# Expert 0's input rows: from full fp32 one-hot products to products of the two parts of X

## The chip, the cores and the metric

One core of one Trainium2 chip runs the program. The metric is the device time of one execution in microseconds (us), as the median of several runs. The engines are TensorE (PE, with its weight loads shown apart as PEld), VectorE (DVE), ScalarE (ACT), GpSimd (POOL) and SyncE (SP, which here only issues transfers).

## The reference, cut to what matters

A batch of 512 tokens with 1024 features passes through four layers: two with attention and a mixture of experts, and two with recurrent mixers and a plain feed-forward net. The change touches the two expert layers. What they compute is

```python
x = layer_norm(x * DN_ALPHA + mixer_out)           # 512 x 1024, f32
group, expert = router(x)                           # top-2 of 32 experts for each token
rows_e = x[tokens that chose e]                     # at most 96 rows kept per expert on the fast path
y_e = (silu(rows_e @ w_gate[e]) * (rows_e @ w_up[e])) @ w_down[e]
x = layer_norm(x * DN_ALPHA + sum of weight * y_e)
```

## The kernel before

The 512 tokens lie in four tiles (t = 0 to 3) of 128 rows in the buffer `X`. Accuracy near full f32 is had from two "parts": a value is rounded by ACT into a part that TensorE takes in a single pass (type fp32r, `one_pass(...)` in the code), and DVE subtracts it from the value, which leaves the second part. Most large products are three single-pass products of such parts. Plain f32 operands are the other way: for such a product the trace has two weight loads and two matmul records per call.

The end of each attention layer is `mixer_out` on TensorE (line 2434). Its last chunk of output columns is done for tiles 0, 1, 2, then tile 0 is transposed (`turn_tile`, L2296), then the chunk is done for tile 3, tile 1 is transposed, the router's logits of tile 0 are formed (`logits`, L2405), tile 2 is transposed, and so on up to the logits of tiles 2 and 3. DVE adds the residual and normalises tile by tile (`residual`, L3163 to L3138; `norm_tile` waits for POOL's reciprocal root, L1025, after `mean_var`, L3126). ACT copies each transposed tile out of two PSUM banks in order (`tiles_T`, L1245); each engine runs its list strictly in order.

Routing comes next, for tiles 0, 1 (q = 0) and then tiles 2, 3 (q = 1): DVE chooses (`choose`, L3403 to L3440), TensorE counts positions (`positions`, L2416, L2417), DVE places (`place`, L3449 to L3468) and writes a one-hot matrix `M["sel"]` of 128 x 96 per tile. `first_rows` (L2429) multiplies X by it, which gives expert 0's rows already transposed in banks 0 and 1, 16 calls for each q; so expert 0 needs no gather. `positions(l, 1)` stands behind `first_rows(l, 0)` in TensorE's list. ACT and DVE take the two banks out in two parts (L1484, L3611), and TensorE starts expert 0's first products (`up_first`, L2081, L2082, L2086), which free the weight halves for the next loads of SP (L906).

The rows of the other experts go through DRAM: POOL scatters X (L1051) and, once DVE's list `used` is ready (L3523), gathers the rows of experts 1, 2 and so on into `M["XE"]` (L1065), two buffers in turn. `clear_rows` (L1058) zeroes both of them; it runs while the mixer's last chunks are under way.

Of the kernel before, what the change touches and what calls it, by code (L numbers as in the profile page):

```python
# [7 lines left out]
ALU = mybir.AluOpType  # L8
ACT = mybir.ActivationFunctionType
# [183 lines left out]
def build(nc, a, out, stages=99):  # L193
    table, where = shape_constants()
    ctx = ExitStack()
    with ctx:
# [429 lines left out]
        M = carve([("XE", (2, D)), ("XET", (2, KD, P)), ("hid", (2, D_EXPERT)), ("YE", (2, D))], 8192)  # L626
        M["XN"] = M["XET"]
        M["XET"] = M["XET"][:, :, :, 0:CAP]
        M["XET_lo"] = XH[:, 0:2, :].rearrange("p b (k c) -> p b k c", k=KD)[:, :, :, 0:CAP]
        M["HT_lo"] = XH[:, 2:4, 0:KE * P].rearrange("p b (k c) -> p b k c", k=KE)[:, :, :, 0:CAP]  # L630
        M["HN"] = XH[:, 2:4, KE * P:2 * KE * P].rearrange("p b (k c) -> p b k c", k=KE)
        M["HT"] = M["HN"][:, :, :, 0:CAP]
        M["both"] = big[:, 15360:15360 + P]
        M["sel"] = big[:, 12288:12288 + T * CAP].rearrange("p (t c) -> p t c", t=T)
# [380 lines left out]
        def _(pool):  # L1015
# [45 lines left out]
            def rows_through(l):  # L1061
# [8 lines left out]
                def scatter(e):  # L1070
# [5 lines left out]
                    ).then_inc(signal(f"y_stored{e % 2}").sem, 16)  # L1076

                pool.wait_ge(signal("used_ready").sem, l + 1)
                pool.wait_ge(signal("rows_sent").sem, 16 * T * TOP_K * (l + 1))
# [40 lines left out]
            if on(3):  # L1120
                pool.wait_ge(full[U["o0_T"][KD - 1].bank], U["o0_T"][KD - 1].n + 1)
                norm_params(a["ln1_g"][0], a["ln1_b"][0])
                clear_rows()
                for t in range(T):
                    norm_rstd(t)
# [9 lines left out]
            if on(5):  # L1135
                pool.wait_ge(full[U["o1_T"][KD - 1].bank], U["o1_T"][KD - 1].n + 1)
                norm_params(a["ln1_g"][1], a["ln1_b"][1])
                clear_rows()
                for t in range(T):
                    norm_rstd(t)  # L1140
# [54 lines left out]
        def _(act):  # L1195
# [44 lines left out]
            def tiles_T(name):  # L1240

                for i, u in enumerate(U[name]):
                    t, b = divmod(i, 2)
                    act.wait_ge(full[u.bank], u.n + 1)
                    act.activation(XT[:, 4 * b:4 * b + 4, t * P:(t + 1) * P], ps(u)[:, :].rearrange("p (k c) -> p k c", k=4), ACT.Copy).then_inc(  # L1245
                        drained[u.bank], 1)
                    act.wait_ge(drained[u.bank], u.n + 1)

            def moments(t):
# [474 lines left out]
            if on(5):  # L1724
                linear("qkv", C["H"], 3 * D, between=raw_bias)
                act.wait_ge(signal("x_normed").sem, signal("x_normed").next(act, 2 * T))
                windows()
                round_chunk(W["odd_o"][1])
                tiles_T("ln11_T")
            if on(6):  # L1730
                experts(1)
            if on(7):
                round_chunk(W["mix_in"][0])
                act.wait_ge(signal("x_normed").sem, signal("x_normed").next(act, T))
                moments(0)
# [304 lines left out]
        def _(pe):  # L2040
# [379 lines left out]
            def first_rows(l, q):  # L2420

                base = U[f"moe{l}"]
                pe.wait_ge(signal("first_marked").sem, signal("first_marked").next(pe))
                for b in range(2):
                    if q == 0:
                        pe.wait_ge(drained[b], base[b])
                    for j in range(4):
                        for t in (2 * q, 2 * q + 1):
                            ins = pe.matmul(psum[b][:, j * CAP:(j + 1) * CAP], X[:, t, :].rearrange("c (h p k) -> c h k p", h=2, k=4)[:, b, j, :], M["sel"][:, t, :],  # L2429
                                            start=(t == 0 and j == 0), stop=(t == T - 1 and j == 3))  # L2430
                    if q == 1:
                        ins.then_inc(full[b], 1)
# [637 lines left out]
        def _(dve):  # L3070
# [87 lines left out]
            def residual_tile(name, c, t, scale):  # L3158
# [5 lines left out]
                dve.wait_ge(drained[u.bank], u.n + 1)  # L3164

            def residual(name, scale):

                for c in range(2):
                    for t in range(T):
                        residual_tile(name, c, t, scale)  # L3170
                        half_stats(t, c)
                        if c == 1:
                            mean_var(t)
                            norm_tile(t)

# [267 lines left out]
            def place(l, q):  # L3443
# [7 lines left out]
                for t in (2 * q, 2 * q + 1):  # L3451
                    ins = dve.tensor_scalar(M["sel"][:, t, :], k("places"), neg_mean[:, t:t + 1], R["M"][:, t, 0:1], ALU.is_equal, ALU.mult)
                ins.then_inc(signal("first_marked").sem, 1)
# [116 lines left out]
            def route(l):  # L3570

                dve.memset(R["LP"], -3e38).then_inc(dve_done.sem, 1)
                dve.wait_ge(dve_done.sem, dve_done.next(dve))
                dve.memset(R["Mc"][:, 0, :], 0.0).then_inc(dve_done.sem, 1)
                dve.wait_ge(dve_done.sem, dve_done.next(dve))
                for q in range(2):
                    choose(l, q)
                    place(l, q)
                scores(l)
                fullest(l)  # L3580
# [731 lines left out]
```

## Time and profile before

| | |
|---|---|
| median of 3 runs | 2994.32 us (2990.87 to 2997.32) |
| the profiled execution | 2994.94 us, of which the span of instructions is 2993.1 us |
| PE / PEld / DVE / ACT / POOL busy | 97% / 75% / 71% / 54% / 12% |
| mean granted TensorE clock | 0.982 |
| transfers | 600.5 MB, mean 201 GB/s |

Busy shares are means over stages with different limits. The granted clock is 1.00 at 2.4 GHz and 0.50 at 1.2 GHz. In a timeline a row may stand for several like instructions that follow each other; then its duration is that of all of them.

### The profile page before, as it was taken

How to read it: one execution, taken by the hardware profiler on the slowest of the kernel's cores; microseconds unless marked ns; L12 is line 12 of the kernel's file. 1: busy time of each engine (PE TensorE's matmuls, PEld its weight loads, DVE VectorE, ACT ScalarE, POOL GpSimd, SP SyncE). 2: the span in 40 equal slices, each digit the busy share in tenths (PEclk: the TensorE clock that was granted, in tenths of full speed). 3: DMA queues.
4: the chain of work that ended last, by engine and by line, in shares of the span. 5: the costliest groups of instructions: out<-in, count | busy, mean ns of one | idle time of the engine just before them, and what ended most of it. 6: DMA issues, size and time to landing. Idle time of an engine off the chain costs nothing.

```text
span 2993.1 us, 38811 instructions
## 1 busy us (share of the span) xinstructions
PE 2895.8 (97%) x14261; PEld 2257.0 (75%) x14261; DVE 2123.5 (71%) x2376; ACT 1604.9 (54%) x1969; POOL 358.4 (12%) x273
## 2 busy tenths in 40 slices
PE   8999899999989999899999999999999999999998
PEld 7668776767768767677677668888888887888886
DVE  3485799999972467899999865674776648676762
ACT  3573588888853464788888743433222226522211
POOL 0000212222220002122222220100000000000000
PEclk9999899999999998999999999999999999999999
DMA  7303799999962125899999844301232223232222
GB/s 273 136 1 113 261 389 405 409 398 400 405 223 85 39 99 226 334 399 398 404 399 406 332 106 99 66 20 64 92 102 95 99 85 99 92 111 93 91 94 84
DMA packets 170900, 600.50 MB, mean 201 GB/s; under 512 B 21697, under 2 KB 71025, under 8 KB 121363
## 3 DMA queue, kind: packets, MB, share of 16 engines
q1 hardware_dynamic: 140432, 541.22, 48.5%
q0 software_dynamic: 19840, 52.60, 4.9%
q10 hardware_dynamic: 10499, 4.91, 0.6%
q8 instruction: 88, 1.44, 0.2%
q14 instruction: 41, 0.34, 0.0%
HBM read 574.15 MB, written 40.37 MB: 205 GB/s over the span
## 4 chain that ended last, share of the span: by engine, by line
PE 73%; DMA 11%; DVE 7%; ACT 5%; issue 3%; POOL 1%; DVEq 0%; SPq 0%; ACTq 0%; POOLq 0%
PE bank L2074 14%; PE bank L2076 14%; PE bank L2075 14%; DMA ring<-w_gate 6%; PE bank L2512 4%; PE bank L2509 4%; DMA ring<-w_up 3%; PE bank L2086 3%; PE bank L2794 2%; PE bank L2528 2%; PE bank L2081 2%; PE bank L2082 2%; PE bank L2138 1%; PE bank L2139 1%; ACT ring_rounded L1479 1%
## 5 line engine op out<-in xcount | busy, mean ns | idle before, releaser
L3601 DVE TENSOR_TENSOR ring_rounded<-ring,big_rounded 128x2048 fp32r<-128x2048 f32 x252 | 567.6, 2288 | 32.0 <-ACT big_rounded L1479 31.0
L1479 ACT ACTIVATE big_rounded<-ring 128x2048 fp32r<-128x2048 f32 x252 | 481.9, 1916 | 44.2 <-DMA ring<-w_up 33.2
L3096 DVE TENSOR_TENSOR ring_rounded<-ring,ring_rounded 128x2048 fp32r<-128x2048 f32 (+2 forms) x118 | 261.4, 2255 | 329.8 <-ACT ring_rounded L1221 329.4
L1221 ACT ACTIVATE ring_rounded<-ring 128x2048 fp32r<-128x2048 f32 (+2 forms) x124 | 226.5, 1876 | 369.3 <-DMA ring<-ffn_w_down 150.1
L3601 DVE TENSOR_TENSOR ring_rounded<-ring,ring_rounded 128x2048 fp32r<-128x2048 f32 x128 | 292.4, 2288 | 43.5 <-ACT ring_rounded L1479 43.1
L1479 ACT ACTIVATE ring_rounded<-ring 128x2048 fp32r<-128x2048 f32 x128 | 245.0, 1917 | 96.5 <-DMA ring<-w_gate 95.5
L2074 PE MATMUL bank<-XT_rounded,ring_rounded 128*128 128x512 f32 (+1 forms) x792 | 295.8, 374 | 0.4 <-DVE XH_rounded L3149 0.4
L2076 PE MATMUL bank<-XT_rounded,ring_rounded 128*128 128x512 f32 (+1 forms) x792 | 292.9, 370 | 0.0
L2075 PE MATMUL bank<-XH_rounded,ring_rounded 128*128 128x512 f32 (+1 forms) x792 | 292.9, 370 | 0.0
L2512 PE MATMUL bank<-ring_rounded,big_rounded 128*128 128x512 f32 x960 | 265.7, 399 | 7.4 <-DVE ring_rounded L3601 6.9
L2075 PE MATMUL bank<-ring_rounded,XH_rounded 128*64 128x512 f32 (+2 forms) x608 | 239.6, 394 | 0.0
L2076 PE MATMUL bank<-ring_rounded,big_rounded 128*128 128x512 f32 (+1 forms) x608 | 235.8, 388 | 0.0
L2512 PEld LDWEIGHTS bank<-ring_rounded,big_rounded 128*128 128x128 f32 x960 | 179.2, 190 | 59.5 <-DVE ring_rounded L3601 22.5
L2074 PE MATMUL bank<-ring_rounded,XT_rounded 128*128 128x512 f32 (+1 forms) x560 | 218.6, 390 | 0.4 <-DVE XH_rounded L4043 0.3
L2075 PE MATMUL bank<-ring_rounded,XT_rounded 128*128 128x512 f32 (+1 forms) x560 | 217.0, 387 | 0.0
L2074 PE MATMUL bank<-big_rounded,XH_rounded 128*64 128x512 f32 (+1 forms) x496 | 199.1, 401 | 5.1 <-DVE XH_rounded L3615 5.1
L2076 PE MATMUL bank<-big_rounded,XH_rounded 128*64 128x512 f32 (+1 forms) x512 | 202.4, 395 | 0.0
L3720 DVE SCALAR_TENSOR_TENSOR big<-bank,chan,big 128x511 f32<-128x511 f32 (+2 forms) x236 | 176.7, 749 | 8.4
L1073 POOL DMA_INDIRECT expert_rows<-big,idx x64 | 88.1, 1377 | 766.4 <-ACT big L1515 739.9
L1023 POOL TENSOR_SCALAR st<-st 128x1 f32<-128x1 f32 (+3 forms) x43 | 14.5, 337 | 1302.7 <-ACT lnp L1589 801.1
L2074 PEld LDWEIGHTS bank<-XT_rounded,ring_rounded 128*128 128x128 f32 x792 | 149.3, 188 | 26.3 <-issue 1.6
L2075 PEld LDWEIGHTS bank<-XH_rounded,ring_rounded 128*128 128x128 f32 x792 | 149.3, 189 | 25.8 <-issue 1.0
(525 smaller groups left out, 5527.1 us busy)
## 6 DMA issues: line engine op xcount, KB each, us to landing
ring<-w_up SPq DMA_DIRECT2D x128, 1024.0 KB, 9.8
ring<-w_down SPq DMA_DIRECT2D x128, 1024.0 KB, 7.7
ring<-w_gate SPq DMA_DIRECT2D x128, 1024.0 KB, 7.9
ring<-ffn_w_up SPq DMA_DIRECT2D x44, 1024.0 KB, 7.0
ring<-ret_gdn_w_in SPq DMA_DIRECT2D x8, 2048.0 KB, 13.1
ring<-ffn_w_down SPq DMA_DIRECT2D x8, 2048.0 KB, 7.7
expert_rows<-lnp POOLq DMA_DIRECT2D x1, 12288.0 KB, 40.3
ring<-odd_w_qkv SPq DMA_DIRECT2D x6, 2048.0 KB, 8.1
```

The source lines that it names most:

```text
L1073: pool.indirect_dma_start(expert_rows, bass.IndirectOffsetOnAxis(ap=used[0:slots_of(e), e:e + 1], axis=0), M["YE"][0:slots_of(e), e % 2, : ...
L1221: act.activation(one_pass(hi(c)[:, ks, :]), raw(c)[:, ks, :], ACT.Copy).then_inc(rounded[c.pair], 1)
L1479: act.activation(one_pass(expert_hi(j)), expert_raw(j), ACT.Copy).then_inc(signal("half_rounded").sem, 1)
L2074: pe.matmul(dst, x_hi, y_hi, start=first, stop=False)
L2075: pe.matmul(dst, x_hi, y_lo, start=False, stop=False)
L2076: return pe.matmul(dst, x_lo, y_hi, start=False, stop=last)
L2086: return pe.matmul(dst, one_pass(x_hi), one_pass(y_lo), start=False, stop=last)
L2509: pe.matmul(psum[b][:, :], one_pass(M["XN"][:, half, 4 * i + kk, :]), one_pass(expert_hi(j)[:, kk, :]), start=(i + kk == 0), stop=False)
L2512: ins = pe.matmul(psum[b][:, :], one_pass(M["XN"][:, half, 4 * i + kk, :]), one_pass(expert_raw(j)[:, kk, :]), start=False, stop=(4 * i + ...
L3096: dve.tensor_tensor(one_pass(w), w, parts(hi(c)[:, ks, :]), ALU.subtract).then_inc(split[c.pair], 1)
L3601: dve.tensor_tensor(one_pass(expert_raw(j)), expert_raw(j), parts(expert_hi(j)), ALU.subtract).then_inc(signal("half_split").sem, 1)
L3720: ins = dve.scalar_tensor_tensor(dst[:, d:S], ps(u)[:, 0:S - d], taps[n - 1 - d], dst[:, d:S], ALU.mult, ALU.add)
```

## The change

ACT rounds each normalised tile of X into a first part `x_hi` (`x_rounded`), and DVE takes the rest into `x_lo` (`x_rest`). The parts lie in buffers that are not yet used at that time (the two row buffers `XE` among them). The one-hot matrix is written as fp32r, and each plain f32 call of `first_rows` becomes two single-pass calls, one for each part. `x_rounded(t)` stands in ACT's list ahead of the copies of tile t for t = 0, 1, 2, and behind all copies for t = 3. `x_rest(t - 1)` stands in DVE's list between `mean_var(t)` and `norm_tile(t)`; `x_rest(3)` stands between `choose(l, 1)` and `place(l, 1)`. Since `XE` now holds parts of tile 2, `clear_rows` moves: POOL runs it after both banks of `first_rows` are complete, ahead of the first gather.

```diff
+        M["XET_all"] = M["XET"].rearrange("p b k c -> p b (k c)")
+        M["x_hi"] = [M["XET_all"][:, 0], M["YE"][:, 0], M["XE"][:, 0], XH[:, 2, :]]
+        M["x_lo"] = [M["XET_all"][:, 1], M["YE"][:, 1], M["XE"][:, 1], XH[:, 3, :]]
@@ POOL, rows_through
+                for b in range(2):
+                    pool.wait_ge(full[b], base[b] + 1)
+                clear_rows()
                 pool.wait_ge(signal("used_ready").sem, l + 1)
@@ POOL, ahead of norm_rstd, both layers
-                clear_rows()
@@ ACT, tiles_T
                 for i, u in enumerate(U[name]):
                     t, b = divmod(i, 2)
+                    if b == 0 and t < T - 1:
+                        x_rounded(t)
                     act.wait_ge(full[u.bank], u.n + 1)
...
+                x_rounded(T - 1)
+
+            def x_rounded(t):
+                act.wait_ge(signal("x_normed").sem, signal("x_normed").next(act))
+                act.activation(one_pass(M["x_hi"][t]), X[:, t, :], ACT.Copy).then_inc(signal("x_rounded").sem, 1)
@@ PE, first_rows
+                pe.wait_ge(signal("x_rest").sem, signal("x_rest").next(pe, 2))
...
-                            ins = pe.matmul(psum[b][:, j * CAP:(j + 1) * CAP], X[:, t, :].rearrange("c (h p k) -> c h k p", h=2, k=4)[:, b, j, :], M["sel"][:, t, :],
-                                            start=(t == 0 and j == 0), stop=(t == T - 1 and j == 3))
+                            for part, rows in enumerate((M["x_hi"][t], M["x_lo"][t])):
+                                ins = pe.matmul(psum[b][:, j * CAP:(j + 1) * CAP], one_pass(rows.rearrange("c (h p k) -> c h k p", h=2, k=4)[:, b, j, :]), one_pass(M["sel"][:, t, :]),
+                                                start=(t == 0 and j == 0 and part == 0), stop=(t == T - 1 and j == 3 and part == 1))
@@ DVE
+            def x_rest(t):
+                dve.wait_ge(signal("x_rounded").sem, signal("x_rounded").next(dve))
+                dve.tensor_tensor(one_pass(M["x_lo"][t]), X[:, t, :], parts(M["x_hi"][t]), ALU.subtract).then_inc(signal("x_rest").sem, 1)
@@ DVE, residual
                             mean_var(t)
+                            if t:
+                                x_rest(t - 1)
                             norm_tile(t)
@@ DVE, route
                     choose(l, q)
+                    if q == 1:
+                        x_rest(T - 1)
                     place(l, q)
```

## Rows read from the trace of the kernel before

**Rows 1.** The profile's page: engine shares of the chain that ended last.

```profile
PE 73%; DMA 11%; DVE 7%; ACT 5%; issue 3%; POOL 1%; DVEq 0%; SPq 0%; ACTq 0%; POOLq 0%
```

**Rows 2.** Chain that ended last, first expert layer: start us, us, what.

```profile
297.26 0.43 PE bank L2416 x2
298.84 7.78 PE bank L2429 x32
306.63 0.43 PE bank L2416 x2
308.35 7.78 PE bank L2429 x32
318.07 0.43 PE bank L2082
342.69 8.27 DMA ring<-w_gate
```

**Rows 3.** Stretches: length; busy (instructions) of PE, PEld, DVE, ACT, POOL; PEclk; DMA share, GB/s.

```profile
299.20:299.40 0.20, 0.20 (x2) 0.20 (x2) 0.20 (x1) 0.20 (x1) 0.00 (x0) 0.83 0.00 0
321.00:323.00 2.00, 2.00 (x7) 1.25 (x6) 2.00 (x2) 0.00 (x0) 1.70 (x2) 0.50 0.22 43
323.00:325.00 2.00, 2.00 (x10) 1.44 (x9) 2.00 (x1) 0.00 (x0) 0.84 (x1) 0.94 0.44 111
400.00:500.00 100.00, 97.83 (x450) 70.62 (x449) 91.05 (x61) 85.72 (x81) 24.13 (x12) 0.98 1.01 400
```

**Rows 4.** Groups by form (weights 128*128, moving 128x96 and so on): count, busy us, mean ns, idle.

```profile
L2521 PE MATMUL bank<-big 128*128 128x512 f32 x120 | 61.2, 591 | 0.0
L2512 PE MATMUL bank<-ring_rounded,big_rounded 128*128 128x512 f32 x960 | 265.7, 399 | 7.4 <-DVE ring_rounded L3601 6.9
L2405 PE MATMUL bank<-router,XT 128*128 128x36 f32 x128 | 14.8, 275 | 0.0
L2405 PEld LDWEIGHTS bank<-router,XT 128*128 128x128 f32 x128 | 14.8, 192 | 0.0
L2512 PEld LDWEIGHTS bank<-ring_rounded,big_rounded 128*128 128x128 f32 x960 | 179.2, 190 | 59.5 <-DVE ring_rounded L3601 22.5
L2075 PEld LDWEIGHTS bank<-ring_rounded,XH_rounded 128*64 128x64 f32 x480 | 64.7, 135 | 40.4
```

**Rows 5.** DVE's timeline, first expert layer, the norm of tile 3 and the start of place(0, 1).

```profile
288.23 0.21 DVE L3126 BATCH_NORM_AGGREGATE st<-st 128x2 f32<-128x12 f32 x1
289.52 1.28 DVE L3136 SCALAR_TENSOR_TENSOR X<-X,st,lnp 128x1024 f32<-128x1024 f32 x1 [1.08 <-POOL st L1025]
307.53 0.16 DVE L3449 COPY st<-bank 128x2 f32<-128x2 f32 x1 [2.73 <-PE bank L2417]
```

**Rows 6.** ACT's timeline, first expert layer: copies of tile 1, the route's exponential.

```profile
287.19 1.23 ACT L1245 ACTIVATE XT<-bank 128x512 f32<-128x512 f32 x2 [5.24 <-PE bank L2296]
309.79 0.22 ACT L1464 ACTIVATE st<-st 128x16 f32<-128x16 f32 x1 [4.69 <-DVE st L3480]
```

**Rows 7.** Groups by form: ACT and DVE passes of 128x1024 into fp32r.

```profile
L1221 ACT ACTIVATE ring_rounded<-ring 128x1024 fp32r<-128x1024 f32 x4 | 4.2, 1060 | 23.4 <-DMA ring<-ffn_w_down 23.4
L3096 DVE TENSOR_TENSOR ring_rounded<-ring,ring_rounded 128x1024 fp32r<-128x1024 f32 x4 | 4.9, 1226 | 13.8 <-ACT ring_rounded L1221 13.8
```

**Rows 8.** PE's timeline around the last tile: transposes of tile 1, transposes of tile 3.

```profile
286.50 1.04 PE L2296 MATMUL bank<-const,X 128*128 128x128 f32 x8
292.18 1.09 PE L2296 MATMUL bank<-const,X 128*128 128x128 f32 x8 [0.32 <-DVE X L3138]
```

**Rows 9.** POOL's and PE's timeline: clearing, gather, its transposes; landing of L1065's gathers.

```profile
243.13 1.83 POOL L1058 MEMSET big<- 96x2048 f32 x1
319.31 2.38 POOL L1065 DMA_INDIRECT big<-expert_rows,idx  x1 [4.22 <-DVE idx L3523]
331.16 1.08 PE L2464 MATMUL bank<-const,big 96*128 96x96 f32 x8
DMA to landing us min/median/max: 4.1/8.8/9.8
```

More of the change, by code:

```diff
@@ L1137, in _ @@
                 norm_params(a["ln1_g"][1], a["ln1_b"][1])
-                clear_rows()
                 for t in range(T):
@@ L1725, in _ @@
                 linear("qkv", C["H"], 3 * D, between=raw_bias)
-                act.wait_ge(signal("x_normed").sem, signal("x_normed").next(act, 2 * T))
+                act.wait_ge(signal("x_normed").sem, signal("x_normed").next(act, T))
                 windows()
@@ L1733, in _ @@
                 round_chunk(W["mix_in"][0])
-                act.wait_ge(signal("x_normed").sem, signal("x_normed").next(act, T))
                 moments(0)
@@ L3451, in place @@
                 for t in (2 * q, 2 * q + 1):
-                    ins = dve.tensor_scalar(M["sel"][:, t, :], k("places"), neg_mean[:, t:t + 1], R["M"][:, t, 0:1], ALU.is_equal, ALU.mult)
+                    ins = dve.tensor_scalar(one_pass(M["sel"][:, t, :]), k("places"), neg_mean[:, t:t + 1], R["M"][:, t, 0:1], ALU.is_equal, ALU.mult)
                 ins.then_inc(signal("first_marked").sem, 1)
```

## The prediction

> **What bounds the kernel now.** I read the page first: TensorE carries 73% of the chain that ended last, transfers 11% [rows 1]. The change touches two short stretches, one in each expert layer, so the chain is read there next. It runs through `first_rows`: 32 records in 7.78 us for q = 0, the positions of q = 1, which stand behind them on TensorE, 32 records in 7.78 us again, then, once ACT and DVE have taken the banks out, `up_first` [rows 2]. The second expert layer repeats this within 0.1 us, so each term below counts twice. Behind it the weights' stream is the bound: the chain turns to a transfer of `w_gate` at 342.69 [rows 2], and the DMA share is 1.01 from 400 to 500 [rows 3]. That stream starts when `up_first` frees the first half, so whatever moves the start of `up_first` moves the whole expert stage, one for one.
>
> Next the granted clock, by stretches. It falls from 1.00 to 0.50 between 299.2 and 299.4 and returns after 323 [rows 3]. So nearly all of `first_rows` runs at 1.2 GHz, and so do the first 13 or so records of `up_first` (0.43 us for a record of 512 columns [rows 2]). TensorE had done its last dense 512-column product before 286.5 [rows 8]; since then it had done only transposes, 36-column logits and the positions.
>
> **The products themselves.** Before, 16 f32 calls for each q leave 32 records. After, 16 calls become 32 single-pass calls, so 32 records. What does one cost? Before: 7.78 / 32 = 0.243 us [rows 2]. Is that the passes or the weight load? The moving side is 96 columns. Plain f32 does pass twice in a record: with 512 columns a record has 591 ns against 399 ns for a single-pass one, 192 ns more, about 512 columns more at 2.4 GHz [rows 4]. But with 36 columns a record still takes 14.8 / 128 = 0.116 us at full clock [rows 4], although two passes of 36 columns are 0.03 us: there the load of 128 weight columns is the floor. Doubled for the half clock that is 0.23, next to the 0.243 seen, while two passes of 96 columns are 0.16 us at 1.2 GHz. The positions, with unbroken weights, take 0.43 / 2 = 0.215 us at the same clock [rows 2]. So the record is bound by the load. And the load of an fp32r weight is no shorter: 190 ns for 128 columns against 192 ns for f32; 64 columns take 135 ns [rows 4], so a column costs (190 - 135) / 64 = 0.86 ns, two cycles, 110 ns for 128 columns, 220 ns at half clock. No row has an fp32r product with so few columns, so I bound it: from 0.215 (positions) to 0.243 us, and I take 0.243, since it has the same stepped weights. Saved by the passes: nothing; at the lower bound 32 x 0.028 = 0.9 us for each q.
>
> A rule weighed: the Trainium skill (FP8 and Floating Point Precision, TensorE Precision Notes) counts true FP32 as four passes, so two parts against one exact operand would be half. The 591 ns of the wide record agree with it, the 0.116 us of the narrow one shows where it stops to matter; what it would give is rival A.
>
> **What is added, and where it lies.** ACT: four `x_rounded` of 128x1024 per layer at 1.06 us; DVE: four `x_rest` at 1.23 us [rows 7].
> - x_rest(0) stands where DVE waits 1.08 us for POOL's root in any case; it costs some 0.2 us, and DVE's wait for the next tile's product takes that up.
> - x_rest(2), ahead of norm_tile(3), is the one that counts. It needs x_rounded(2), and that stands in ACT's list behind the copies of tile 1, which wait for TensorE's transposes at 286.50 and run from 287.19 for 1.23 us, to 288.42 [rows 6, 8]. So x_rounded(2) ends at 288.42 + 0.03 + 1.06 = 289.51. DVE is ready for x_rest(2) at 288.23 + 0.21 = 288.44 [rows 5] and waits; it runs 289.56 to 290.79, and the norm of tile 3 starts at 290.83 instead of 289.52 [rows 5]: **+1.31 us**. POOL's root is ready long before. x_rest(1) suffers the same wait, 1.3 us, but DVE's idle time ahead of the residual of tile 3 and its wait for x_rounded(2) take it up.
> - Queued behind that wait on DVE is all of the routing: the norm of tile 3, `choose`, `place`. TensorE waits with it, for tile 3's transposes at 292.18 [rows 8]. Nothing in between has slack: DVE goes from `choose` to `place` waiting only for the positions.
> - x_rest(3), 1.23 us, lies in the 2.73 us that DVE waits for the positions of q = 1 [rows 5]. Cost nothing; without that cover, 1.23 us.
> - x_rounded(3) moves ACT's later weight rounding by 1.06 us; ACT then idles 4.69 us ahead of the exponential [rows 6]. Nothing.
> - `clear_rows` leaves POOL's list ahead of the norms, where it was off the path. In its new place it starts at the end of the products, 308.35 + 7.78 = 316.1 [rows 2], and takes 1.83 us, to some 318.1; the gather waits for DVE's list in any case and starts at 319.31. Its landing is needed by the transposes at 331.16 [rows 9]. Behind it in POOL's list stand the gathers and scatters only. Nothing.
>
> Sum: 2 x 1.31 = 2.6 us more. On the profiled execution: 2994.94 + 2.6 = 2997.5; it lies 0.6 above the median of the three runs, 2994.32, and on that the forecast is **2997**.
>
> **Rivals.**
> A. *A record gets cheaper* because the passes decide after all. For: a wide f32 record does show its second pass. Against: the narrow rows above, and the load time of fp32r. Price: each q in 3.89 us. For q = 0, positions can start when `choose` ends, and DVE's wait shrinks from 2.73 to the 1.27 of x_rest(3): 1.46 saved. For q = 1 all 3.89. So 5.35 - 1.31 = 4.04 us for each layer, 8.1 in all: 2986. The Trainium skill (TensorE: Matmul & The Clock Gate, Fast Weight Load) would go further, with a quick load of 128 weights for types other than FP32; 190 ns for fp32r against 192 for f32 speaks against it. Chance 0.13.
>
> B. *The clock falls earlier*, the slower side. TensorE now has 0.32 us idle before tile 3's transposes [rows 8]; with the change 1.6 us. If the clock falls before the logits of tiles 2 and 3 (32 records behind those transposes, now 32 x 0.116 = 3.7 us), they take 32 x 0.215 = 6.9 us, from 294.4 to 301.3, and the positions of q = 0, wanted at 297.26 [rows 2] + 1.31 = 298.6, stand behind them: 2.7 us, and 0.2 for themselves at half clock. With the 1.31 that is 4.2 for each layer: 2994.3 + 8.4 = 3002.7. It decides if the clock falls more than about 2 us sooner than at 299.3. For: longer idleness ahead. Against: it fell 12.8 us after the last dense product [rows 3, 8], about the same in the second layer, and that product does not move. Chance 0.12.
>
> C. *The clock returns later* in `up_first`, since TensorE's array does less in `first_rows` (96 columns for each load, not 192). It returned some 5 to 6 us after the 512-column records began (the row at 318.07 is an early one [rows 2, 3]). A record of 512 columns costs 0.43 instead of 0.23, so each us later costs about 0.5; 3 us later in both layers gives 2997 + 3 = 3000. Chance 0.07.
>
> D. *The change does not hide its clearing*: POOL's memset beside DVE's busy stretch, or behind a late semaphore, delays the gather. A gather lands at most 9.8 us after its issue, so at 329.1, and is needed at 331.16 [rows 9]; it decides from 2 us late on. At 3 us late it gives 1 us for each layer: 2999. Chance 0.03.
>
> **How the numbers follow.** Forecast 0.65, A 0.13, B 0.12, C 0.07, D 0.03. A measurement of this kernel tells 0.2%, 6 us, from no change. Faster by more: A, 0.13. Slower by more, above 3000.3: B and part of C, 0.15. The rest, 0.72, is within. The forecast's own range is 2993 (0.9 us saved for each q in both layers, less 2.6) to 3000; run to run the kernel spreads by 3 us either way. The range over the cases leaves out most of A: 2987 to 3003.5.
>
> **What would show it.** In the changed profile: 32 records for each q in about 7.8 us at a granted clock of 0.50; DVE idle about 1.1 us ahead of x_rest(2), released by ACT; norm of tile 3 starting 2.6 us behind `mean_var` rather than 1.3; DVE's wait ahead of `place(l, 1)` reduced by x_rest(3) to about 1.5 us; the memset ending before the list is ready. The prediction is wrong if the records come at 0.12 to 0.16 us, or if the clock falls before the positions.

## The result, and the profile after

The changed kernel took 3002.96 us (median of 7 runs, 2999.92 to 3013.06), the kernel before beside it 2991.59 us (7 runs): a ratio of 1.0032, 95% interval 1.0021 to 1.0043, or 9.6 us more (the medians themselves are 11.4 us apart; the sums below go by the ratio). The profiled execution took 3003.21 us (span 3001.4) against 2994.94 before, 8.3 us more. The forecast of 2997 was some 6 us short; the range (to 3003.5) just holds the median, because it took in the slower rival B, and the loss is over the 0.2% that a measurement tells.

Line numbers moved: the transposes are L2308, the logits L2417, the positions L2428 and L2429, `first_rows` L2443, expert 1's transposes L2478, the norm L3150 and L3152, POOL's two small operations for the root L1026 and L1028. New are `x_rounded` (ACT, L1260) and `x_rest` (DVE, L3183).

TensorE's timeline of the changed kernel, first expert layer, tile 1's transposes, then tile 3's and what follows (start us, us, engine line, tile, count, idle time before and its releaser):

```profile
286.48 1.04 PE L2308 MATMUL bank<-const,X 128*128 128x128 f32 x8
...
293.36 1.09 PE L2308 MATMUL bank<-const,X 128*128 128x128 f32 x8 [1.52 <-DVE X L3152]
294.29 5.93 PE L2417 MATMUL bank<-router,XT 128*128 128x36 f32 x32
300.03 0.67 PE L2428 MATMUL bank<-big,ones 128*128 128x64 f32 x2
```

Tile 1 is where it was, within 0.02 us [rows 8]. Tile 3's transposes come 1.18 us later and TensorE idles 1.52 us ahead of them, not 0.32. Then the logits of tiles 2 and 3 (32 records) take 5.93 us, where the forecast wanted 3.7, and the positions start 2.77 us later than before [rows 2]. The stretches of the granted clock say why (columns as in [rows 3]):

```profile
295.00:295.20 0.20, 0.20 (x4) 0.20 (x4) 0.17 (x2) 0.20 (x1) 0.03 (x1) 1.00 0.00 0
295.20:295.40 0.20, 0.20 (x4) 0.20 (x3) 0.17 (x2) 0.17 (x2) 0.00 (x0) 0.80 1.01 184
295.40:295.60 0.20, 0.20 (x3) 0.20 (x2) 0.17 (x2) 0.20 (x1) 0.00 (x0) 0.50 0.43 123
```

It fell to 1.2 GHz at 295.3, four us sooner than before, and in the middle of the logits. The second expert layer is worse. TensorE's timeline there; it had done its last dense product at 1145.92:

```profile
1153.30 1.97 PE L2308 MATMUL bank<-const,X 128*128 128x128 f32 x8 [2.02 <-DVE X L3152]
```

and the clock, which fell at 1152.1, while TensorE idled ahead of those transposes:

```profile
1151.90:1152.10 0.20, 0.00 (x0) 0.00 (x0) 0.16 (x2) 0.00 (x0) 0.00 (x0) 0.91 0.48 205
1152.10:1152.30 0.20, 0.00 (x0) 0.00 (x0) 0.20 (x1) 0.00 (x0) 0.00 (x0) 0.50 1.54 655
```

The transposes take 1.97 instead of 1.09 us, and the logits behind them 6.88 instead of 3.66. The products themselves are as they were: the chain of waits of the changed kernel has 7.75 us for each q, against 7.78 [rows 2].

```profile
302.05 7.75 PE bank L2443 x32
...
311.53 7.75 PE bank L2443 x32
```

The second thing that the forecast did not have stands in the timelines of DVE and POOL. DVE, first expert layer, the norm of tile 3:

```profile
288.88 0.21 DVE L3140 BATCH_NORM_AGGREGATE st<-st 128x2 f32<-128x12 f32 x1
289.54 1.25 DVE L3183 TENSOR_TENSOR big_rounded<-X,big_rounded 128x1024 fp32r<-128x1024 f32 x1 [0.45 <-ACT big_rounded L1260]
290.71 1.27 DVE L3150 SCALAR_TENSOR_TENSOR X<-X,st,lnp 128x1024 f32<-128x1024 f32 x1
```

Tile 3's norm starts at 290.71 (forecast 290.83). The same place one tile earlier starts at 284.79 with 0.44 us of waiting for POOL behind `x_rest(1)`, and POOL's rows for tiles 1 and 2 are:

```profile
276.62 1.15 POOL L1026 TENSOR_SCALAR st<-st 128x1 f32<-128x1 f32 x1 [4.75 <-DVE st L3140]
277.86 0.55 POOL L1028 TENSOR_TENSOR st<-st,const 128x1 f32<-128x1 f32 x1
282.90 0.19 POOL L1026 TENSOR_SCALAR st<-st 128x1 f32<-128x1 f32 x1 [4.50 <-DVE st L3140]
283.18 1.58 POOL L1028 TENSOR_TENSOR st<-st,const 128x1 f32<-128x1 f32 x1
```

Whichever of the two small operations starts while `x_rest` runs takes one us longer: 1.15 instead of 0.19, or 1.58 instead of 0.55. At tile 3 of this layer the second one starts at 289.52, just ahead of the pass, and takes 0.54 us.

`up_first` starts 3.14 us later in the first layer. In the second it starts 11.12 us later, of which 5.67 us were there at tile 1's transposes, so 5.45 us are new. Together 8.6 us, and the execution is 8.3 us longer.

### The profile page after: what moved, and what is told of

It reads as the page before. It is cut to its first block, busy times and chain, and to the rows that moved or that the text cites. A ratio compares the mean times of both kernels' runs of the same rounds, so it can differ in the third digit from the quotient of the medians.

```text
span 3001.4 us, 38830 instructions
## 1 busy us (share of the span) xinstructions
PE 2899.3 (97%) x14261; PEld 2260.9 (75%) x14261; DVE 2134.0 (71%) x2384; ACT 1613.1 (54%) x1977; POOL 359.5 (12%) x273
## 4 chain that ended last, share of the span: by engine, by line
PE 73%; DMA 10%; DVE 7%; ACT 5%; issue 4%; POOL 1%; DVEq 0%; SPq 0%; ACTq 0%; POOLq 0%
PE bank L2086 14%; PE bank L2088 14%; PE bank L2087 14%; DMA ring<-w_gate 6%; PE bank L2526 4%; PE bank L2523 4%; PE bank L2098 3%; DMA ring<-w_up 3%; PE bank L2542 2%; PE bank L2808 2%; PE bank L2093 2%; PE bank L2094 2%; ACT ring_rounded L1492 2%; PE bank L2150 1%; PE bank L2151 1%
## 5 line engine op out<-in xcount | busy, mean ns | idle before, releaser
L3624 DVE TENSOR_TENSOR ring_rounded<-ring,big_rounded 128x2048 fp32r<-128x2048 f32 x252 | 567.7, 2289 | 33.7 <-ACT big_rounded L1492 32.9
L1026 POOL TENSOR_SCALAR st<-st 128x1 f32<-128x1 f32 (+3 forms) x43 | 15.9, 370 | 1306.1 <-ACT lnp L1602 802.4
```

The costliest lines, as they stand in the source:

```text
L3624: dve.tensor_tensor(one_pass(expert_raw(j)), expert_raw(j), parts(expert_hi(j)), ALU.subtract).then_inc(signal("half_split").sem, 1)
```

## The experiments

Where an experiment's kernel starts its layer some us earlier or later, distances from the start of tile 1's transposes (the end of the last dense product) are compared. This table has the two expert layers of each profiled execution, and the ratio of all runs to the kernel before. "Fall" is the distance at which the granted clock fell, "tile 3" and `up_first` are starts. One execution stands for each kernel's distances: those of e1, e3 and e8 were the fastest of their runs, those of e5 and e13 among the slowest.

| kernel | tile 3 | fall | logits of tiles 2, 3 | `up_first` | ratio |
|---|---|---|---|---|---|
| before | 5.68 / 5.68 | 12.8 / 12.4 | 3.66 / 3.66 | 30.9 / 30.9 | 1 |
| the change | 6.88 / 7.38 | 8.8 / 6.1 | 5.93 / 6.88 | 34.0 / 36.3 | 1.0032 [1.0021, 1.0043] |
| e1_act_order | 7.16 / 7.31 | 6.9 / 8.1 | 6.88 / 6.88 | 36.1 / 35.5 | 1.0038 [1.0023, 1.0053] |
| e2_rest_late | 6.36 / 6.41 | 6.5 / 8.1 | 6.88 / 6.23 | 35.1 / 33.8 | 1.0023 [1.0013, 1.0033] |
| e3_split_only | 6.89 / 7.37 | 13.0 / 9.5 | 3.66 / 5.76 | 32.0 / 34.3 | 1.0024 [1.0014, 1.0035] |
| e4_products_only | 5.68 / 5.68 | 11.4 / 11.6 | 3.66 / 3.66 | 30.9 / 30.9 | 1.0001 [0.9991, 1.0011] |
| e5_one_part | 5.68 / 5.68 | 10.9 / 9.7 | 3.66 / 4.06 | 26.0 / 26.3 | 0.9961 [0.9948, 0.9975] |
| e8_after_dense_t3 | 6.88 / 7.37 | 12.6 / 11.7 | 3.66 / 3.82 | 31.9 / 32.9 | 1.0013 [1.0004, 1.0023] |
| e10_rests_moved | 5.78 / 5.84 | 10.3 / 11.7 | 3.66 / 3.66 | 31.4 / 31.4 | 1.0007 [0.9998, 1.0016] |
| e11_rest_beside | 6.57 / 6.56 | 7.8 / 6.1 | 6.59 / 6.88 | 34.2 / 35.3 | 1.0017 [1.0007, 1.0028] |
| e12_bf16_parts | 5.78 / 5.85 | 13.0 / 11.7 | 3.66 / 3.66 | 27.0 / 27.3 | 1.0019 [1.0008, 1.0029] |
| e13_bf16_filled | 5.78 / 5.85 | 10.2 / 11.7 | 3.68 / 3.66 | 27.0 / 27.3 | 1.0001 [0.9992, 1.001] |

### The split or the products: e3_split_only and e4_products_only

e3 keeps the split, its waits and the moved clearing, and forms the products in f32 as before. e4 does the reverse: no `x_rest` on DVE, and the second part is a buffer of zeros, so that the second part's share of expert 0's rows is left out.

```diff
 e3, PE, first_rows (and the one-hot stays f32)
-                            for part, rows in enumerate((M["x_hi"][t], M["x_lo"][t])):
-                                ins = pe.matmul(psum[b][...], one_pass(rows...), one_pass(M["sel"][:, t, :]), ...)
+                            ins = pe.matmul(psum[b][...], X[:, t, :]..., M["sel"][:, t, :], ...)
 e4, PE, first_rows (and both x_rest calls are gone)
-                            for part, rows in enumerate((M["x_hi"][t], M["x_lo"][t])):
+                            for part, rows in enumerate((M["x_hi"][t], M["x_lo"][0])):
```

> The changed kernel with its split, its clearing and all its waits, but with the products and the one-hot matrix in plain f32 as before. Theory W: same as the changed kernel, 3003 us, and the same early fall of the clock. Rival P (the products in fp32r cost): back towards 2992 to 2995 us.

> The single-pass products without the price of the split: DVE takes no rest; the second product of each pair reads a buffer of zeros instead of the rest, so expert 0's rows lack the second part of X. ACT still rounds, off the path. Theory W with the load as the floor of a record: 32 records for each q in 7.75 us as in both kernels, clock falls behind the logits, whole time that of the kernel before, 2992 us plus or minus 3. Rival A (passes decide): 3.9 us for each q and about 2981 us.

e3 took 3001.83 us and e4 2995.9 us, with the kernel before at 2994.43 beside them. e4's chain has the products at

```profile
302.55 7.75 PE bank L2447 x32
...
312.10 7.75 PE bank L2447 x32
```

So two single-pass records cost what one f32 call costs, the products change nothing, and the whole loss is the split and what waits for it. e4 also keeps the moved clearing, so that costs nothing either. Rival A is out. One part of e3's expectation missed: in its first layer the clock did not fall early (13.0 us, logits in 3.66 us).

### What a record costs: e5_one_part

e4 without its second part: 16 records for each q, and X's second part is left out of expert 0's rows.

```diff
-                            for part, rows in enumerate((M["x_hi"][t], M["x_lo"][0])):
+                            for part, rows in enumerate((M["x_hi"][t],)):
```

> The kernel with zeros for the rest (DVE takes none), with the second product of each pair left out: 16 records for each q; expert 0's rows have only the first part of X. Theory W with the weight load as the floor: 0.24 us a record at half clock, so 3.9 us for each q; for q = 0 DVE's wait ahead of place(1) shrinks by about 1.6, for q = 1 3.9 us are saved: 5.5 us for each layer, 2983 us. Rival (the clock returns later because TensorE does less): as much of it is lost in up_first, 2988 to 2992 us.

It took 2982.15 us, ratio 0.9961 [0.9948, 0.9975]. TensorE's timeline of this kernel:

```profile
302.95 3.97 PE L2447 MATMUL bank<-big_rounded 128*128 128x96 f32 x16 [0.93 <-DVE big_rounded L3475]
```

Half the records (0.248 us each) is half the time, and 12 us of the kernel. The stretch is worth attacking, then, but by the count of records (or what a record costs), which the change left at 32.

### ACT's wait: e2_rest_late and e1_act_order

e2 takes `x_rest(2)` away from tile 3's norm and puts it ahead of `x_rest(3)`. e1 leaves it, and has ACT round tile t + 1 ahead of the copies of tile t, so that the rounded tile is there in time.

```diff
 e2, DVE, residual (and route: x_rest(T - 2) ahead of x_rest(T - 1))
-                            if t:
+                            if t and t < T - 1:
                                 x_rest(t - 1)
 e1, ACT, tiles_T
-                    if b == 0 and t < T - 1:
-                        x_rounded(t)
+                    if b == 0 and t < T - 2:
+                        if t == 0:
+                            x_rounded(0)
+                        x_rounded(t + 1)
```

> The changed kernel, with the rest of tile 2 taken by DVE between choose(1) and place(1), not ahead of the norm of tile 3. Theory W (the loss is the wait ahead of the norm of tile 3, and the earlier fall of the clock that this idleness brings): tile 3's transposes start within 0.5 us of the kernel before (292.2 and, measured from tile 1's transposes, 5.7 us behind them), the clock falls behind the logits again, the logits of tiles 2 and 3 take 3.7 us and not 5.9 or 6.9, and the start of up_first comes 2 to 3 us earlier than in the changed kernel in the first layer, 4 to 5 us in the second: about 2993 to 2997 us. Rival P (the single-pass products or the late clearing cost the time): the whole time stays at 3003.

> The changed kernel with ACT rounding tile t + 1 ahead of the copies of tile t (for t = 0 and 1), so that x_rounded(2) no longer stands behind tile 1's copies. Theory W: x_rest(2) starts without the 0.45 us wait, but DVE's pass and POOL's root then start together, and POOL's root is slowed as it is ahead of the norm of tile 1 (0.7 us of wait left behind the pass), so the norm of tile 3 still starts some 2.1 us behind mean_var and not 1.3; the clock still falls early in at least one layer; 2999 to 3003 us. Rival (the wait on ACT is the whole delay): norm of tile 3 starts as before and the time is 2994.

e2 missed: 3001.05 us where the time of before was expected. The norm of tile 3 waits 1.08 us for POOL again, as before, yet tile 3 is still 0.7 us late. DVE's timeline shows what had come to it from the tiles ahead:

```profile
284.84 1.23 DVE L3183 TENSOR_TENSOR big_rounded<-X,big_rounded 128x1024 fp32r<-128x1024 f32 x1 [0.39 <-ACT big_rounded L1260]
286.50 1.28 DVE L3150 SCALAR_TENSOR_TENSOR X<-X,st,lnp 128x1024 f32<-128x1024 f32 x1 [0.44 <-POOL st L1028]
291.89 1.29 DVE L3150 SCALAR_TENSOR_TENSOR X<-X,st,lnp 128x1024 f32<-128x1024 f32 x1 [1.08 <-POOL st L1028]
```

In the kernel before, DVE's idle time ahead of tile 3's residual was

```profile
286.78 0.69 DVE L3163 SCALAR_TENSOR_TENSOR X<-X,bank 128x512 f32<-128x512 f32 x1 [1.07 <-PE bank L2076]
```

What tiles 1 and 2 lost to their passes and to POOL is more than these 1.07 us. In e1 DVE doesn't wait for ACT at tile 3, and still nothing is won (3004.65 us):

```profile
289.22 1.23 DVE L3185 TENSOR_TENSOR big_rounded<-X,big_rounded 128x1024 fp32r<-128x1024 f32 x1
291.15 1.28 DVE L3152 SCALAR_TENSOR_TENSOR X<-X,st,lnp 128x1024 f32<-128x1024 f32 x1 [0.71 <-POOL st L1028]
```

Without ACT's wait the pass falls on POOL's first operation, and DVE waits 0.71 us for POOL afterwards. ACT's wait and POOL's stall take each other's place.

### POOL beside DVE, by itself: e10_rests_moved and e11_rest_beside

e10 takes all passes off the norms. e11 differs from it in one thing: `x_rest(0)`, whose input was rounded long ago, stands between `mean_var(3)` and `norm_tile(3)`.

```diff
 e10, DVE, residual                              e11: x_rest(0) if t == 3, ahead of norm_tile(t)
-                            if t:
-                                x_rest(t - 1)
                             norm_tile(t)
+                            if t == 2:
+                                x_rest(0)
 both, DVE, route, between choose and place
-                    if q == 1:
-                        x_rest(T - 1)
+                    if q == 0:
+                        x_rest(1)
+                    else:
+                        x_rest(2)
+                        x_rest(3)
```

> The changed kernel with all of DVE's passes for the second parts taken off the norms: x_rest(0) stands behind norm_tile(2), where DVE waits 1.07 us for TensorE's product in the trace of before; x_rest(1) stands between choose and place of q = 0; x_rest(2) and x_rest(3) stand between choose and place of q = 1. ACT's roundings stay where they are. Theory (the loss is what stands ahead of tile 3's norm, in two portions: ACT's wait plus a POOL that is slow beside DVE's pass): tile 3's transposes come 5.7 to 5.9 us behind tile 1's, as before (5.68), POOL's two small operations take 0.19 and 0.55 us again, the norm waits 1.08 us, the clock falls 12 to 13 us behind the last dense product, the logits of tiles 2 and 3 take 3.7 us, and the kernel loses only what x_rest(1) lacks in cover, 0.5 to 1 us for each layer: ratio 1.0000 to 1.0008. Rival (ACT's roundings slow POOL or the copies too): tile 3 still comes over 0.5 us late and the ratio stays at 1.002 or above.

> As e10_rests_moved, but x_rest(0), whose input was rounded long ago, stands between mean_var(3) and norm_tile(3), so that one pass of DVE of 1.23 us, with no wait of its own, lies beside POOL's two small operations. Theory (a tensor_tensor pass of DVE holds POOL up for its length): POOL's first operation takes about 1.15 instead of 0.19 us or its second about 1.5 instead of 0.55, the norm of tile 3 still waits 0.7 us behind the pass and starts about 1.9 us behind mean_var instead of 1.08, so tile 3's transposes come 0.7 to 0.9 us late; the clock may fall earlier; ratio 1.000 to 1.002. Rival (POOL works beside it): the norm starts 1.25 us behind mean_var, tile 3 comes 0.15 us late.

e10: 2996.17 us against 2994.59, ratio 1.0007, as expected; the early fall is gone. e11: 2999.59 us, ratio 1.0017. POOL's timelines at tile 3, of e10 and then of e11:

```profile
288.89 0.19 POOL L1026 TENSOR_SCALAR st<-st 128x1 f32<-128x1 f32 x1 [5.70 <-DVE st L3140]
289.17 0.54 POOL L1028 TENSOR_TENSOR st<-st,const 128x1 f32<-128x1 f32 x1
```

```profile
288.42 1.15 POOL L1026 TENSOR_SCALAR st<-st 128x1 f32<-128x1 f32 x1 [5.60 <-DVE st L3140]
289.65 0.54 POOL L1028 TENSOR_TENSOR st<-st,const 128x1 f32<-128x1 f32 x1
```

and DVE's of e11:

```profile
288.29 1.23 DVE L3183 TENSOR_TENSOR big_rounded<-X,big_rounded 128x1024 fp32r<-128x1024 f32 x1
290.23 1.28 DVE L3150 SCALAR_TENSOR_TENSOR X<-X,st,lnp 128x1024 f32<-128x1024 f32 x1 [0.71 <-POOL st L1028]
```

One pass with no wait of its own costs 1.23 + 0.71 us where a wait of 1.08 us stood, 0.8 us net, and the logits took 6.6 and 6.9 us. That a pass beside POOL's small operations adds itself to them, rather than hiding them, is shown. In e10 ACT's roundings run as in the change, and POOL's operations are quick: it is DVE's pass, not ACT's.

### The clock: e8_after_dense_t3, e6_before_dense, e9_before_dense_all

e8 is the changed kernel with three plain f32 products of 256 columns, whose result nobody reads, in the idle time ahead of tile 3's transposes. e6 puts such products into the kernel before, ahead of the positions (one) and of the first `first_rows` (two); e9 fills every gap up to the second one.

```diff
+            def dense(l, n):
+                u = U[f"ln1{l}_T"][3]
+                pe.wait_ge(drained[u.bank], u.n + 1)
+                for _ in range(n):
+                    pe.matmul(ps(u)[:, 0:256], ident, const[:, 0:256], start=True, stop=True)
 e8, mixer_out
                 logits(l, 1)
+                dense(l, 3)
                 turn_tile(normed, X, 3, "x_normed")
 e6, mixer_out (e9: also 1 ahead of tile 3, 3 behind first_rows(l, 0), 1 ahead of first_rows(l, 1))
                 logits(l, 3)
+                dense(l, 1)
                 for q in range(2):
                     positions(l, q)
+                    if q == 0:
+                        dense(l, 2)
                     first_rows(l, q)
```

> The changed kernel with three plain f32 products of 256 columns (about 1.4 us of TensorE at full clock, results unused) between the logits of tile 1 and the transposes of tile 3, where TensorE idles 1.5 and 2.0 us. Theory W: the idleness is what makes the clock fall early, so with it filled the clock stays at 1.00 through the logits of tiles 2 and 3 (3.7 us) and up_first starts 2 us earlier in the first layer, 3 to 4 us in the second; about 2998 us. Rival (the clock falls at its time whatever TensorE does in this gap): logits still 5.9 and 6.9 us, 3003 us.

> The kernel before, with plain f32 products of 256 columns (0.47 us each at full clock, results unused): one between the logits of tile 3 and the positions of q = 0, two between these positions and first_rows(0), where TensorE waits for DVE. If dense work in these gaps holds the clock at 1.00 through first_rows(0), a record costs 0.12 us and up to 8 us for each layer are gained: 2980 us. If not (first_rows itself is too thin to hold it): 2992 to 2994 us.

> The kernel before with such products in every gap of TensorE from the logits on: one ahead of tile 3's transposes, one ahead of the positions, two ahead of first_rows(0), three behind it, one ahead of first_rows(1). If the clock stays at 1.00: up_first starts 6 to 9 us earlier than in the kernel before, 2978 to 2984 us. If it falls in spite of them, the three products behind first_rows(0) delay the positions of q = 1 by about 2.8 us: 2997 us.

e8 took 2998.47 us, ratio 1.0013. Its timeline of TensorE:

```profile
291.46 1.54 PE L2452 MATMUL bank<-const 128*128 128x256 f32 x6
293.15 1.09 PE L2308 MATMUL bank<-const,X 128*128 128x128 f32 x8
294.08 3.66 PE L2417 MATMUL bank<-router,XT 128*128 128x36 f32 x32
```

Tile 3 is as late as in the change (6.88 us behind tile 1), and the logits are back at 3.66 us. By the ratios 5.7 of the 9.6 us hang on the early fall (1.0032 less 1.0013; the intervals leave some 4 us to either side); by `up_first` in the profiled executions it is 5.5 (8.6 us late in the change, 3.1 in e8, whose profiled execution took 2994.78 us).

e6 (2994.83 us, ratio 1.0009) and e9 (2994.86 us, 0.9999) gained nothing. e9 tells why, for it holds `first_rows` at either level. Two stretches of it, the first within q = 0 and the second within q = 1:

```profile
302.20:306.20 4.00, 4.00 (x19) 4.00 (x19) 2.06 (x13) 2.67 (x2) 2.79 (x3) 0.50 0.90 358
311.20:315.20 4.00, 4.00 (x19) 4.00 (x18) 2.84 (x14) 0.92 (x3) 2.50 (x3) 1.00 0.36 145
```

19 records in 4 us at 1.2 GHz, and 19 in 4 us at 2.4 GHz. The weight loads of these records, grouped by form, give the same row in both stretches:

```profile
L2429 PEld LDWEIGHTS bank<-big,X 128*128 128x128 f32 x18 | 4.3, 329 | 0.0
```

329 ns a load at either level, where a load for the logits takes 192 ns at full clock [rows 4]. The chain of waits has the positions just ahead of the second at full speed, and 32 records of `first_rows` in 7.78 us as always:

```profile
308.81 0.19 PE bank L2416 x2
309.00 0.21 PE bank L2417 x2
...
310.13 7.78 PE bank L2429 x32
```

So these products don't run with the granted clock, and holding it through them gives nothing back. That fillers could save the logits in e8 is no contradiction: those take 0.116 us a record at one level and 0.215 at the other.

### A cheaper record: e12_bf16_parts and e13_bf16_filled

e12 is e10 with bf16 for both parts and the one-hot. It leaves out what two bf16 parts can't hold of a value of X for expert 0. e13 adds seven filler products ahead of expert 1's transposes.

```diff
 e12
-    one_pass(rows.rearrange("c (h p k) -> c h k p", h=2, k=4)[:, b, j, :]), one_pass(M["sel"][:, t, :])
+    half_width(rows, D).rearrange("c (h p k) -> c h k p", h=2, k=4)[:, b, j, :], half_width(M["sel"][:, t, :], CAP)
 e13, also, PE, rows_T
+                    if isinstance(e, int) and e == 1:
+                        wait_use(drained, 0, e)
+                        for _ in range(7):
+                            pe.matmul(psum[0][:, 0:256], ident, const[:, 0:256], start=True, stop=True)
```

> As e10_rests_moved, but both parts and the one-hot are bf16 instead of fp32r: ACT writes bf16(X), DVE writes bf16 of the rest. This leaves out what two bf16 parts can't hold of each value of X for expert 0 (the bits below some 16). Again 32 records for each q. It asks whether a record of these products is bound by the load of its 128 weight columns whatever the type. If a column costs the same two cycles: 7.7 us for each q, ratio as e10. If the narrower type loads in half the cycles, a record comes to about 0.12 us at the half clock (or to the 96 columns' own pass, 0.08 to 0.1 us at 1.2 GHz), first_rows takes 3 to 4 us for each q, and as with e5_one_part some 6 us for each layer come back: ratio about 0.996.

> As e12_bf16_parts (it leaves out the same: what two bf16 parts can't hold of X for expert 0), with seven plain f32 products of 256 columns (some 3.6 us at full clock) in front of expert 1's transposes, in the stretch in which TensorE waits for the gathered rows (4.93 us in the first expert layer, 3.67 in the second). In e12_bf16_parts TensorE reached that wait 3.9 us sooner than before, the gather landed no sooner (transposes 44.6 us behind tile 1's, before 44.7), the clock fell in the wait and was 0.50 until about 340, and expert 2's transposes came 67.4 us behind tile 1's against 64.1 before. Theory (that 3.3 us is the clock that fell in the new wait): with the wait filled the clock stays at 1.00 through it, expert 2's transposes come 64 to 65 us behind tile 1's, and the kernel returns to about the time of before, ratio 0.9995 to 1.0008. Rival (the weights' stream, which stood still while nothing was freed, is what came late): filling changes neither, ratio 1.0015 or more.

TensorE's timeline of e12:

```profile
299.06 2.58 PE L2447 MATMUL bank<-big 128*128 128x96 bf16 x32 [1.28 <-DVE big L3477]
...
305.08 0.74 PE L2432 MATMUL bank<-big,ones 128*128 128x96 f32 x2 [3.44 <-DVE big L3465]
...
330.89 1.55 PE L2482 MATMUL bank<-const,big 96*128 96x96 f32 x8 [4.93 <-DMA big<-expert_rows,idx]
```

32 records in 2.58 us, 0.081 us each, at a granted clock of 0.50 from 299.3 on; 96 columns at 1.2 GHz are 0.080 us, so a bf16 record comes at the pace of its moving columns. Their loads take 138 ns instead of 329. What held the others at 0.243 us goes with the four-byte types; the weights' type, their step in bytes and the one-hot's type changed together here, so which of them it is stays open. But the kernel took 3001.14 us, ratio 1.0019 [1.0008, 1.0029], although `up_first` started 3.9 and 3.6 us sooner: part of what TensorE won it spent waiting for DVE (3.44 us ahead of the positions of q = 1), and at the end of `up_first` it waited 4.93 us for the gathered rows of expert 1. Its chain of waits:

```profile
313.97 4.68 DMA expert_rows<-X,idx
...
319.57 11.27 DMA big<-expert_rows,idx
330.89 1.55 PE bank L2482 x8
```

The gather took 11.27 us from issue to landing. In the kernel before, the same gather, issued at 319.31, took 5.4 us:

```profile
big<-expert_rows,idx POOLq DMA_INDIRECT x1, 5.4
```

That the weights' stream, which now started sooner, is what slowed it is argued only. Nor did the gather start sooner: 33.3 us behind tile 1's transposes, 32.8 before. It stood behind the scatters of q = 1, whose last was issued 27.7 us behind them, 27.6 before. The transposes stand 44.6 us behind tile 1's, no earlier than before (44.7). In that wait the clock fell again:

```profile
333.00:337.00 4.00, 2.83 (x8) 1.85 (x8) 3.36 (x4) 3.88 (x3) 0.93 (x1) 0.50 0.52 197
337.00:339.00 2.00, 2.00 (x6) 1.31 (x5) 2.00 (x2) 2.00 (x2) 0.00 (x0) 0.50 0.00 0
```

and expert 2's transposes came 67.4 and 66.3 us behind tile 1's, against 64.1 and 63.9. e13 filled the wait and took 2993.78 us, ratio 1.0001 [0.9992, 1.001]. Its profiled execution, at 2999.3 us a slow one of its eleven, holds both cases. In the second layer 0.68 us of the wait were left:

```profile
1185.62 3.18 PE L2481 MATMUL bank<-const 128*128 128x256 f32 x14
1189.49 1.22 PE L2486 MATMUL bank<-const,big 96*128 96x96 f32 x8 [0.68 <-DMA big<-expert_rows,idx]
```

and its stretch

```profile
1189.00:1196.00 7.00, 5.34 (x28) 4.13 (x29) 4.26 (x5) 5.75 (x6) 0.93 (x1) 1.00 0.70 276
```

is at full clock, with expert 2's transposes 63.4 us behind. In the first layer the gather landed later, 2.82 us of wait stayed, the clock fell, and expert 2's came 68.1 us behind. So e12's loss is the clock that fell in the new wait, and with it kept the kernel is where it was before: the gather is the next bound. No kernel here that computes all of it beat the kernel before; e5 shows what a halved count would bring.

## Why the prediction was right or wrong

- **The products: the value right, its working not.** 32 records for each q at 0.242 us, so nothing saved (e4), and the count is what costs (e5). But the prediction got its 0.23 by doubling the 0.116 of the 36-column records for the half clock. e9 shows 0.24 at either level, so the doubling met the value by chance. The load is what fits: a single pass of 96 columns needs far less, and the loads last 329 ns at either level (e9) and 138 ns in the narrower type (e12). Why they last that long is not shown. The rule on four passes did not bear here.
- **x_rest(2) ahead of tile 3's norm: right in the first layer.** The norm started at 290.71 for 290.83, tile 3's transposes 1.18 us late for 1.31, since the end of ACT's rounding set the time. But DVE idled 0.45 us ahead of the pass and not 1.1: it came to `mean_var(3)` 0.65 us late (288.88 for 288.23) from the tiles ahead, which the forecast had put at nothing. In the second layer tile 3 was 1.70 us late.
- **"POOL's root is ready long before": wrong.** It held at tile 3 of the first layer only, where POOL's second operation started 0.02 us ahead of the pass (289.52 and 289.54) and took its usual 0.54 us. In the second layer it started 0.06 us behind the pass (1149.04 and 1148.98) and took 1.58. At tiles 1 and 2 POOL stood still beside the pass, and DVE waited 0.72 and 0.44 us on top. The prediction costed x_rest(0) at 0.2 us and saw both taken up by DVE's idle time. e2, e1 and e11 show they were not all taken up: with ACT's wait removed either way, tile 3 stays 0.7 to 1.6 us late. In the second layer the chain of waits runs through POOL at tile 3:

```profile
1149.04 1.58 POOL st L1028
```

- **The clock: the step that failed.** The forecast took it that the clock falls 12.8 us after the last dense product whatever lies between, and gave the early fall, rival B, 0.12. It fell after 8.8 and 6.1 us. B's mechanism is what came, and with it `up_first` was 3.1 and 5.5 us late, where B had 4.2 for each layer. That B's total of 3002.7 lies beside the median of 3002.96 is partly luck: one layer cost less and the other more. The table shows what the row of before could not. With tile 3 at 5.7 to 5.9 us the fall came at 9.7 to 13.0 in all twelve cases (before, e4, e5, e10, e12, e13). With tile 3 at 6.4 or later and the gap unfilled it came at 6.1 to 9.5 in nine of ten cases (the change, e1, e2, e3, e11), and at 13.0 in one (e3, first layer). The two groups nearly touch, at 9.7 (e5) and 9.5 (e3), and in e5's second layer the fall reached the logits (4.06 us) with tile 3 on time. One row of a fall has no spread, and the step that lengthened the idleness was the very one that the forecast had costed.
- **Rival C: not needed.** `up_first`'s first products stayed at half clock 5.5 and 4.0 us from their start, against 5.9 and 5.5 before.
- **Hidden steps: right.** DVE's wait ahead of `place(l, 1)` shrank from 2.73 to 1.42 us; ACT idled 5.74 us ahead of the exponential; the clearing ended before the list was ready:

```profile
319.40 1.80 POOL L1061 MEMSET big<- 96x2048 f32 x1 [1.14 <-PE bank L2443]
322.51 2.34 POOL L1068 DMA_INDIRECT big<-expert_rows,idx  x1 [1.30 <-DVE idx L3544]
```

- **The sum.** 2.6 us forecast, 9.6 measured. By e8 some 5.5 to 5.7 us are the early fall. The rest is the delay, put at 2.6: e8's `up_first` is 1.1 and 2.0 us late, 3.1 in all, and its ratio gives 3.9.

## What to carry to other kernels

Before replacing plain f32 products by single-pass ones, read the narrowest record at hand: where it takes far longer than its moving columns, only fewer or cheaper records help, and more clock may not. An engine's idle time is cover only if nothing that shares it gets slower, so a pass put beside another engine's small operations has to be looked for in both timelines. And where TensorE works thinly, a us more of idleness ahead of a block can bring the clock down across all of it: price a delay there with the block at half clock, unless several rows show that the fall stays.

## What the runs showed of the hardware

- A DVE `tensor_tensor` of 128x1024 with both inputs in SBUF, once under way, held up POOL's operations of one element per partition until it ended: 0.19 to 1.15 us and 0.55 to 1.58 us in the change, 0.19 to 1.15 in e11 with nothing else changed. The Trainium skill (SBUF — State Buffer, Who interferes with whom) states that such a `tensor_tensor` contends with GpSimd's reads, and that the order of issue decides who blocks. These traces agree: where POOL's operation started 0.02 us ahead of the pass (the change, first layer, tile 3) it took 0.54 us, and the pass 1.25 instead of 1.23. The prediction had not weighed it.
- `first_rows` took 0.243 us for a record at granted clocks of 0.50 and of 1.00 (e9), where 36-column records of f32 took 0.215 and 0.116. Its loads took 329 ns at both levels, the logits' 192 ns at full clock and 333 ns at half (the change). Its weights are read with a step of four columns; so are those of expert 1's transposes (L2464), which at full clock take about 1.1 us for 8 [rows 9], with loads of 215 ns. What sets the two apart was not tried, and stays open.
- The type of the weights: fp32r as slow as f32 (7.75 and 7.78 us for 32 records, loads of 330 and 329 ns), bf16 at 0.081 us for a record of 96 columns at 1.2 GHz, with loads of 138 ns. The Trainium skill (TensorE: Matmul & The Clock Gate, Fast Weight Load) gives the quick load to 128 weights of any type but FP32: the bf16 rows agree with it, and the fp32r loads are as slow as those of FP32.
- Where no fillers stood in between, the granted clock fell between 6.1 and 13.0 us behind the last dense product, with the same work on TensorE and 0.3 to 2.0 us of idle time ahead of tile 3, and it fell in e12's wait of 4.93 us as well. What exactly decides the moment stays open: e3's first layer kept the clock for 13.0 us with tile 3 as late as in the change. That the early fall costs what it does is shown by e8; that the longer idleness brings it is what the table bears out, case by case, and no more.
